# Attention trunk: the last value projection cut in pieces, layer 0's p projection brought forward, both placed between the heads of the second group

## What is computed

```python
x = layer_norm(a*x + 0.5*swiglu(x, ...))        # ffn
x = layer_norm(a*x + mixer_attention(x, ...))   # attention, below
x = layer_norm(a*x + 0.5*swiglu(x, ...))        # ffn
x = x + sigmoid(x @ ple_w_gate[0]) * (p[0] @ ple_w_proj[0])

def mixer_attention(x, w_in, b_f, w_out, rel_bias):
    h = x @ w_in     # q, k, v of 8 heads; q, k, v of 8 more; 8 forget logits
    # group 1: softmax(q k^T / 8 + rel. bias, causal) v
    # group 2: softmax(q k^T / 8 + c_t - c_s, causal) v,  c = cumsum(log sigmoid(f))
    return concat(o_a, o_b) @ w_out
```

## Time and profile before

| | before |
|---|---|
| median of 3 runs | 1063.08 us |
| lowest, highest | 1062.24, 1063.96 us |
| profiled execution, span | 1066.6 us |
| TensorE busy with matmuls | 1046.8 us (98%) |
| VectorE, ScalarE busy | 611.0 us (57%), 447.1 us (42%) |
| mean granted TensorE clock | 0.979 |

### The profile page before, as it was taken

The page is one execution under the profiler, slowest core; times in us unless marked ns, Lnnn a source line. Parts: engine busy times, 40 slices in busy tenths (PEclk is TensorE's granted clock), DMA queues, the critical chain, the costliest instruction groups (busy, mean ns, idle before and its releaser), DMA issues.

```text
span 1066.6 us, 12641 instructions
## 1 busy us (share of the span) xinstructions
PE 1046.8 (98%) x4770; PEld 857.8 (80%) x4770; DVE 611.0 (57%) x705; ACT 447.1 (42%) x516; POOL 39.5 (4%) x53
## 2 busy tenths in 40 slices
PE   7999999999999899999999999999999899999998
PEld 5888888787878688888888888888888688888886
DVE  5645455864434755445586554545678765454574
ACT  5434344245433444434444444444254354344441
POOL 2100000100000100000010000000111100000010
PEclk9999999999957999999999999999999999999999
DMA  8855655446302576465546755545266575655531
GB/s 276 290 200 178 211 184 173 131 146 191 111 15 67 170 259 213 158 199 177 182 173 222 247 178 197 196 158 201 95 207 230 176 265 184 210 183 171 197 119 40
DMA packets 128914, 191.46 MB, mean 180 GB/s; under 512 B 5320, under 2 KB 95432, under 8 KB 128752
## 3 DMA queue, kind: packets, MB, share of 16 engines
q1 hardware_dynamic: 125952, 180.37, 50.5%
q0 software_dynamic: 2928, 10.61, 3.0%
HBM read 189.90 MB, written 1.06 MB: 179 GB/s over the span
## 4 chain that ended last, share of the span: by engine, by line
PE 91%; DVE 4%; DMA 2%; ACT 1%; issue 1%; SPq 0%; POOL 0%; DVEq 0%
PE gu L340 19%; PE gu L342 18%; PE gu L341 18%; PE acc L340 9%; PE acc L342 9%; PE acc L341 9%; PE tp L398 4%; DVE g_lo L913 2%; PE acc L542 2%; ACT g_hi L690 1%; DMA rawB<-in_ffn_w_up 1%; PE acc L539 1%; DMA rawB<-in_sgu_w_in 1%; DVE xT_lo L913 0%; DMA rawB<-in_sgu_w_out 0%
## 5 line engine op out<-in xcount | busy, mean ns | idle before, releaser
L340 PE MATMUL gu<-g_hi,xT_hi 128*128 128x512 f32 x928 | 364.4, 393 | 4.8 <-DVE xT_lo L913 3.3
L342 PE MATMUL gu<-g_hi,xT_lo 128*128 128x512 f32 x928 | 361.8, 390 | 0.0
L341 PE MATMUL gu<-g_lo,xT_hi 128*128 128x512 f32 x928 | 361.2, 389 | 0.0
L340 PEld LDWEIGHTS gu<-g_hi,xT_hi 128*128 128x128 f32 x928 | 174.2, 188 | 42.6 <-DVE xT_lo L913 4.2
L342 PEld LDWEIGHTS gu<-g_hi,xT_lo 128*128 128x128 f32 x928 | 174.2, 188 | 36.6
L341 PEld LDWEIGHTS gu<-g_lo,xT_hi 128*128 128x128 f32 x928 | 174.3, 188 | 35.5 <-issue 0.2
L739 ACT ACTIVATE stage<-gu 128x256 f32<-128x256 f32 x88 | 33.8, 384 | 377.6 <-PE gu L342 377.6
L913 DVE TENSOR_TENSOR g_lo<-rawA,g_hi 128x2048 fp32r<-128x2048 f32 (+1 forms) x63 | 142.1, 2256 | 82.6 <-ACT g_hi L690 82.6
L913 DVE TENSOR_TENSOR g_lo<-rawB,g_hi 128x2048 fp32r<-128x2048 f32 (+1 forms) x63 | 141.9, 2252 | 19.3 <-ACT g_hi L690 19.3
L1012 DVE SCALAR_TENSOR_TENSOR stage<-stage,gu 128x256 f32<-128x256 f32 x88 | 37.0, 421 | 194.4 <-ACT stage L739 194.4
L340 PE MATMUL acc<-d_hi,hT_hi 128*128 128x512 f32 x352 | 144.4, 410 | 0.0
(11 more groups left out here) (159 smaller groups left out, 711.5 us busy)
## 6 DMA issues: line engine op xcount, KB each, us to landing
rawD<-in_ffn_w_down SPq DMA_DIRECT2D x44, 1024.0 KB, 4.8
rawA<-in_ffn_w_gate SPq DMA_DIRECT2D x43, 512.0 KB, 3.7
rawA<-in_ffn_w_up SPq DMA_DIRECT2D x43, 512.0 KB, 4.7
rawB<-in_ffn_w_gate SPq DMA_DIRECT2D x43, 512.0 KB, 4.1
rawB<-in_ffn_w_up SPq DMA_DIRECT2D x43, 512.0 KB, 5.3
rawA<-in_attn_w_in SPq DMA_DIRECT2D x12, 512.0 KB, 4.3
rawB<-in_attn_w_in SPq DMA_DIRECT2D x12, 512.0 KB, 4.8
rawA<-in_ple_w_gate SPq DMA_DIRECT2D x8, 512.0 KB, 5.5
```

The costliest lines, as they stand in the source:

```text
L340: pe.matmul(dst, hi[b], w_hi[b], start=first and b == 0, stop=False)
L341: pe.matmul(dst, hi[b], w_lo[b], start=False, stop=False)
L342: done = pe.matmul(dst, lo[b], w_hi[b], start=False, stop=last and b == len(hi) - 1)
```

## The change

Four things are done.

1. p of layer 0 is transposed in the attention, between ("turn", 1, 1) and ("g", 2, 1), as entries ("pT", 0) and ("pT", 1), instead of in the second ffn. Half 1's goes into the bank that ("turn", 1, 1) has just filled.
2. The heads of the first group sit one or two entries earlier, heads 1 and 2 now directly behind each other. The last value chunk (c = 5) is cut in a front (12 products) and a back (12 products) for each half, with head 7, 8, 9 and 10 behind a piece each.
3. The p projection's weights come as a chunk of their own (chunk 6, with 2 of 4 rows of each part used), so that the output chunks are 7 and 8. The projection is done as 4 pieces of 6 products (`proj`) after heads 11, 12, 13 and 14, into `acc[1]`; ScalarE copies each piece to `bias_tab` (called `proj0`) at the next head's entry, and rounds output chunk 7 there in halves of a part. VectorE makes the `g_lo` of chunk 7 at heads 12 and 14. `acc[1]` is then free two heads later, so the transposes of the first group's results move from heads 13 and 14 to heads 15 and 16, the latter waiting for the copy of the last piece.
4. The ple phase of layer 0 has no p projection and no `rawD` chunk any more; it reads `proj0`. The load of the sgu's bias into `bias_tab` waits until that phase is over.

The core of the diff:

```diff
@@ ATTN_ORDER
-    ("g", 2, 0), ("turn", 1, 1), ("g", 2, 1), ("cT",),
-    ("g", 3, 0), ("head", 0), ("g", 3, 1), ("turn", 3, 0), ("head", 1),
...
+    ("g", 2, 0), ("turn", 1, 1), ("pT", 0), ("pT", 1), ("g", 2, 1), ("cT",),
+    ("g", 3, 0), ("head", 0), ("g", 3, 1), ("turn", 3, 0), ("head", 1), ("head", 2),
...
+    ("g front", 5, 0), ("turn", 4, 1), ("head", 7), ("g back", 5, 0), ("head", 8),
+    ("g front", 5, 1), ("head", 9), ("g back", 5, 1), ("head", 10),
+] + [("head", n) for n in range(HEADS + 3, 2 * HEADS + 2)] + [("oT", 0), ("oT", 1)]
+PROJ_AT = HEADS + 3
@@ tensor
+                    def proj(q):
+                        h, j = q // 2, q % 2
+                        if q == 0:
+                            pe.wait_ge(split_a, g0 + 6)
+                            pe.wait_ge(split_b, g0 + 6)
+                        if q < 2:
+                            pe.wait_ge(tok_ready, x0 + j + 1)
+                        else:
+                            pe.wait_ge(proj_taken, q - 1)
...
+                        elif e[0] == "pT":
+                            h = e[1]
+                            pe.wait_ge(p_loaded, 16)
+                            transposes(h, t0 + tp_of[e][1], [p_tok[:, h, P * b:P * b + P] for b in range(2)])
...
-                            if n in (13, 14):
-                                h = n - 13
-                                pe.wait_ge(tok_ready, x0 + h + 1)
+                            if n in (15, 16):
+                                h = n - 15
+                                pe.wait_ge(proj_taken, h + 3)
...
+                            if PROJ_AT <= n < PROJ_AT + 4:
+                                proj(n - PROJ_AT)
@@ tensor, ple
+                        if n == 1 and i == 1:
                             d_product(d0, d0 % 2, 0, pT_hi[:, 0], pT_lo[:, 0], first=True, last=True)
-                        if n == 2:
+                        if n == 2 and i == 1:
@@ scalar, head n (behind the exponentials of n and the probsT copy of n-1)
+                            if PROJ_AT < n <= PROJ_AT + 4:
+                                q = n - PROJ_AT - 1
...
+                                copy(proj0[:, q // 2, q % 2, :], acc[1][:, q % 2, :]).then_inc(proj_taken, 1)
+                            if PROJ_AT <= n < PROJ_AT + 4:
+                                part, rows = (n - PROJ_AT) // 2, (n - PROJ_AT) % 2
+                                done = hi_rows(g0 + 7, part, slice(2 * rows, 2 * rows + 2))
+                                if rows == 1:
+                                    done.then_inc((high_a, high_b)[part], 1)
@@ vector, head n
+                            if n in (PROJ_AT + 1, PROJ_AT + 3):
+                                lo_g(g0 + 7, (n - PROJ_AT - 1) // 2)
-                            if n in (15, 16):
-                                h = n - 15
+                            if n in (16, 17):
+                                h = n - 16
@@ gpsimd
-                if ln == 2:
-                    pool.dma_start(bias_tab[:, :], sgu_b_in[0].partition_broadcast(P)).then_inc(sgu_bias_ld, 16)
...
+                if ln == 2:
+                    pool.wait_ge(tok_ready, bases[3]["x"] + 4)
+                    pool.dma_start(bias_tab[:, :], sgu_b_in[0].partition_broadcast(P)).then_inc(sgu_bias_ld, 16)
```

More of the change, by code:

```diff
@@ L70, in attn_tp_uses @@
             banks = [(e, e[2])]
+        elif e[0] == "pT":
+            banks = [(e, e[1])]
         elif e[0] == "oT":
@@ L101, in phase_bases @@
     out = []
-    for kind, _, s in PHASES:
+    for kind, i, s in PHASES:
         out.append(dict(now))
         now = {k: now[k] + per[kind][k] for k in now}
-        if kind == "ffn" and s == 2:
+        if len(out) - 1 == P_PHASE:
             now["t"] += 1
             now["v"] += 1
+        if kind == "ple" and i == 0:
+            now["d"] -= 1
     return out, now
@@ L118, in build @@
     for k, (kind, _, _) in enumerate(PHASES):
-        pair_firsts |= {bases[k]["g"] + q for q in {"ffn": (), "attn": (6,), "sgu": (4,), "ple": (0,)}[kind]}
+        pair_firsts |= {bases[k]["g"] + q for q in {"ffn": (), "attn": (7,), "sgu": (4,), "ple": (0,)}[kind]}
     def g_used(m):
@@ L183, in build @@
         bias_rev = v_att
+        proj0 = bias_tab[:, :].rearrange("p (h j n) -> p h j n", h=2, j=2)
         with ExitStack() as region:
@@ L257, in g_source @@
             if kind == "attn":
-                w, c = (attn_w_in[0], c) if c < 6 else (attn_w_out[0], c - 6)
+                if c == 6:
+                    v = ple_w_proj[0].rearrange("(b p) (j n) -> p b j n", p=P, n=512)[:, part]
+                    return [(slice(j, j + 1), slice(0, 512), v[:, j:j + 1]) for j in range(2)]
+                w, c = (attn_w_in[0], c) if c < 6 else (attn_w_out[0], c - 7)
             elif kind == "sgu":
@@ L296, in _ @@
                 g0, d0 = bases[k]["g"], bases[k]["d"]
-                chunks = {"ffn": NCH, "attn": 8, "sgu": 6, "ple": 2}[kind]
+                chunks = {"ffn": NCH, "attn": 9, "sgu": 6, "ple": 2}[kind]
                 def load_next(c, part):
@@ L565, in values @@
                                   start=False, stop=True).then_inc(pv_done, 1)
+                    def proj(q):
[7 more added lines that the diff above has]
+                            pe.wait_ge(proj_taken, q - 1)
+                        slot = (g0 + 6) % 2
+                        done = product(acc[1][:, j, :], [pT_hi[:, h, b, :] for b in range(2)],
+                                       [pT_lo[:, h, b, :] for b in range(2)],
+                                       [g_hi[:, slot, 4 * b + j, :] for b in range(2)],
+                                       [g_lo[:, slot, 4 * b + j, :] for b in range(2)])
+                        done.then_inc((proj_full, g_done)[j], 1)
                     for e in ATTN_ORDER:
@@ L1002, in _ @@
                 B = bases[k]
-                f0 = sum(kind in ("ffn", "ple") for kind, _, _ in PHASES[:k])
+                f0 = sum(kind == "ffn" or (kind == "ple" and layer == 1) for kind, layer, _ in PHASES[:k])
                 g0, d0, u0, t0, v0, a0, x0, r0, ln0 = (B[q] for q in ("g", "d", "u", "t", "v", "a", "x", "r", "ln"))
```

135 lines of the change are left out of this document (90 added, 45 removed).

## The result

| | before | changed |
|---|---|---|
| median | 1063.88 us (20 runs) | 1067.27 us (20 runs) |
| lowest, highest | 1060.37, 1066.87 us | 1064.28, 1073.10 us |
| ratio of the medians | | 1.0041, 95% interval 1.0029 to 1.0054 |
| profiled execution, span | 1066.6 us | 1065.1 us |
| its mean granted clock | 0.979 | 0.995 |

The change costs 3.4 us. The forecast was that it costs 0.75, 1063.8 us; the range of 1060 to 1073.5 holds the measured time, and slower was given the largest chance (0.47). There is something odd in the table, though: by the medians the kernel lost 3.4 us, by the two profiled executions it won 1.5. Both are true, and the reason for it is the main finding here.

What follows compares the result with a forecast made beforehand. TensorE was taken to bound the kernel, by its work, waits and clock. The terms -18.5 + 5.7 + 2.65 + 1.6 + 0.7 + 5.7 + 3.9 - 1.0 = +0.75 on 1063.08 gave about 1063.8 us, range 1060 to 1073.5.

Steps and rivals of the forecast that it cites:

- I carry the difference over to it: Base of the sum: made against the profiled 1066.6 us, with the median's 3.5 us lower value taken as a constant difference.
- The -18.5: Clock regained in the attention heads and first output products, if the clock never falls there: 16.1 plus 2.4 us less.
- the fall between heads 10 and 11: Slower rival: two heads without a 512-column product lose the clock before the first piece; +9.3 us, 1073; chance 0.35.
- Products brought in: The p projection's 24 products, now between heads, add 2 x 2.85 = 5.7 us on TensorE.
- The bank of p's transposes: Near 236 us, half 1's transposes wait for VectorE to empty their bank behind a `g_lo`: +2.65 us.
- The clock in that wait: The clock falls in the wait for the bank, 3.4 us of products at half clock: +1.6 us, ends 0 and 3.2.
- Heads 1 and 2: Directly behind each other, they make TensorE wait for head 1's exponentials: +0.7 us, ends 0.4 and 1.7.
- Waits behind `g_lo`: In the late heads: 0.7 before head 13's transposition, 4.5 at the first group's transposes, 0.5 at the output product; +5.7 us.
- Clock in the tail: Half clock from the 4.5 us idle time through the last heads and first output products: +3.9 us, ends 0 and 5.
- ple: 5.7 us of products leave layer 0's ple, but gate product (0,1) needs `xT_lo`: only -1.0 us, ends -0.8 and -3.
- That the tail keeps its clock: Faster rival: the clock survives the idle time behind the last heads, so 3.9 us fall away: 1059.9 us; chance 0.12.
- That ple gives back all: Faster rival: the chain behind gate product (0,1) has slack, so another 4.7 us go: 1059.1 us; chance 0.08.

Runs made afterwards that it cites:

- the pieces one earlier: The changed kernel with the four p projection pieces one head earlier, behind heads 10 to 13: 1066.10 us.
- the tail: The changed kernel with VectorE's second `g_lo` of chunk 7 one head later and ScalarE's last piece copy ahead of head 15's exponentials: 1059.57 us.
- run 9: The changed kernel measured once more, with no edit: 1066.56 us.
- the run with ple alone: The kernel before, with layer 0's p projection left out of ple and nothing put in its place: 1063.62 us, ratio 1.0002.
- run 8: The changed kernel with the edit of the tail, p's half 1 transposed ahead of head 0, and chunk 7's `g_lo` in four halves: 1056.52 us.
- run 6: The kernel before with only the changed kernel's head order and cut value chunk, no p projection in the attention: 1063.88 us, ratio 1.0005.
- run 11: The kernel of run 8 with all four pieces one head earlier and VectorE's division of the first group's results earlier: 1055.51 us.
- runs 8 and 12: One kernel measured twice, the second time without an edit and on another chip: 1056.52 us, then 1055.44 us.

## Why the prediction came out as it did

The forecast had the mechanisms and nearly all sizes right, and was low by 3.4 us, since it put them on the wrong base. The signs that it had named all came: the wait for the copy to `kT` (2.52), the clock of 1.00 from 295 to 315, one wait of 4 to 5 us for `bias_tab` (4.41), and the wait for `xT_lo` in ple (1.72).

**The step that failed: "the median of the runs is 3.5 lower, and I carry the difference over to it".** That treats the difference as a constant. It was clock, and the same clock that the change wins back. The -18.5 was worked out from 40.9 us at half clock in the heads. The middle run of the kernel before has 34 in all: 7 us less to win, at 18.5/40.9 = 0.45 each 3.1. With -15.4 in place of -18.5 the sum is +3.9, and 1063.88 + 3.9 = 1067.7; measured is 1067.27. The 3.5 itself is misread too: it sets a span against times, and the span of a run is 2.2 to 2.6 us less than its time. The profiled execution would have a time of about 1069.0, 5.1 above the median of 20, and 44.3 - 34 = 10 us at half clock by 0.47 are 4.8 of it. The page had shown the mean clock (0.979) and three times of runs below the profiled one's span; that the one explained the other could have been asked, and the range of that term should have been given.

That slower had the largest chance was in part luck. 0.35 of its 0.47 stood for the fall between heads 10 and 11, which did not set the median; the forecast's own spread gave slower 0.12.

Against its own profile the sum was too high, not too low: +0.75, and the spans say -1.5. From the turn at 236 to the first output product the forecast's terms make +1.65 (all up to the tail's 1.9 - 0.5), and the stretch grew from 94.33 to 96.59, by 2.3. From there to the layer norm's transposes behind the output products (351.72 and 352.10) it shrank by 1.5, since the clock was back 2.0 us into the output products instead of 5.3. In the next stretch, to ple, it shrank by 1.9, of which 3.4 x 0.45 = 1.5 is the fall at 353 that is not in this execution. The change does nothing there: of the four profiles of the two kernels two have that fall (the first of before, the second of the changed one) and two do not.

Term by term:

- *Products brought in*, +5.7: a head with its piece takes 3.93 us, 2.47 + 1.46; 4 x 1.46 = 5.8. The estimate of 3.1 by the Trainium skill (TensorE: Matmul & The Clock Gate, Back-to-back issue gap) is contradicted again: 5.8/24 is 0.24 us for a product, not 0.131.
- *The bank of p's transposes*, +2.65: 2.52, ended by VectorE's copy to `kT` behind the `g_lo`, as foretold. The run that moved it won it back, less 1.05.
- *The clock in that wait*, +1.6 with ends 0 and 3.2: it is not a value but a toss. The wait of 2.51 to 2.52 us is in four profiles; in two of them (the changed kernel's first and the pieces one earlier) 3.4 us at half clock follow, in two (the tail, the changed kernel again) none.
- *Heads 1 and 2*, +0.7: 0.56.
- *Waits behind `g_lo`*, 0.7 + 4.5: 0.70 + 4.41, with the chain as foretold, and both shown by taking them away (0.7 by the halves, 4.4 by the tail, where the `g_lo` and the copy moved together).
- *Clock in the tail*, +3.9: it fell during the idle time, at 327.6; from 328.50 to 332.47 and for 2.0 us of output products it was at half, (4.0 + 2.0) x 0.45 = 2.7. In run 9's profile the output products were at half clock for 5.3 us, (4.0 + 5.3) x 0.45 = 4.2. Taking the wait away won 2.9 to 3.6 beyond the wait itself.
- *ple*, -1.0: -0.5 to -1.3, depending on the profile of before it is held against. Shown by the run with ple alone.

**The rivals.** The fall between heads 10 and 11, given 0.35, is real but rare: it is seen in one profile, of a near kernel, and could explain the 3 of 20 runs of the changed kernel at 0.989 to 0.990 and 1071.5 to 1073.1 us; that it fell there in these was not seen. The price of 1073 fits them. I had weighed it as one outcome for the kernel, and it is one for some executions. That the tail keeps its clock is not the case in the changed kernel, and is the case once its wait is gone. That ple gives back all is excluded.

## What to carry to other kernels

Before a sum rests on a stretch at half clock, find out how long that stretch is in the middle run: take the mean clock of each run, or a second profile; the one profile here was among the three longest of a hundred. A step that is moved out of a wait-bound phase wins only what that phase was late by (0.5 us of 5.7 here); its worth is what it does at its new place. And when work goes into a stretch where three engines hand over to each other at every head, cut its side work to the length of a head: one elementwise operation of 2.3 us ahead of the maximum, with the copy that TensorE wants queued behind the exponentials, cost 4.4 us of waiting, and 7 to 8 us with the clock that went with it.

## What the runs showed of the chip

**A clock fall is an event with a chance, not a rule of the program.** The same wait of 2.5 us cost it in two profiles of four; the same two layer norm waits of 1.2 and 0.8 us near 350 us cost it in the first profile of before and not in the second, and the other way round in the changed kernel. The Trainium skill says (TensorE: Matmul & The Clock Gate, Part 1: The HAM clock gate) that the monitor of the clock runs free of the kernel, so that one kernel meets it at another point in each run. These profiles are in line with that; none of them shows the monitor itself.

**It also falls where the profile shows no idle time.** In both profiles of before it fell while TensorE was busy for 5.00 of 5.00 us (waiting in its pipeline counts as busy), in heads of narrow matmuls (at 295.0 and 294.1), and in run 8 at 300.55 likewise. The same section names idle time as what brings the low clock; by that alone the kernel before would keep its clock through the heads and be some 16 us faster. The measurement decides. What does decide it here stays open: after the last 512-column product it took 3.2 us to the fall in run 6, 3.5 in run 8 and 4.9 and 5.0 in the kernel before, and in run 11 8.2 us passed without one. No experiment separated the share of wide products from the mix of instructions.

**Price of the half clock:** 11.0 us of span for 23.9 us more of it (one kernel, runs 8 and 12), 0.46 each; 9.3 us of time for 20 over the runs of the kernel before, 0.47. The prediction's 0.45 agrees.
